# 128 instead of 64 tokens with gathered experts, and the choice of experts by head, among 112 pairs, with keys looked up in half precision

## The chip, the core and the metric

The kernel runs on one core of a Trainium2 chip. TensorE (PE) multiplies matrices, VectorE (DVE), ScalarE (ACT) and GpSimd (POOL) work on tensors, SyncE (SP) issues the large loads; sixteen DMA engines serve the core. The metric is the device time of one execution in microseconds (us), less is better. The median of three runs is quoted.

## The reference

Four layers of mixers and feed-forward blocks come first, then a block of sparse attention and a layer called `peer`, which the change is in. There are 512 tokens of width 1024. Each token chooses, in each of 8 heads, 16 of 16384 experts; an expert is one row of `u` and one of `v`.

```python
def peer(hn, w_q, subkeys, u, v):
    ...
    q = (xt @ w_q).reshape(T, H, 2, PEER_QDIM // 2)
    s = jnp.einsum('thcd,cnd->thcn', q, subkeys).astype(jnp.float32)
    s1, i1 = lax.top_k(s[:, :, 0], K)
    s2, i2 = lax.top_k(s[:, :, 1], K)
    cand = (s1[..., :, None] + s2[..., None, :]).reshape(T, H, K * K)
    sc, ci = lax.top_k(cand, K)
    e1 = jnp.take_along_axis(i1, ci // K, axis=-1)
    e2 = jnp.take_along_axis(i2, ci % K, axis=-1)
    idx = e1 * PEER_NKEYS + e2
    g = jax.nn.softmax(sc, axis=-1)
    ...
        a = jnp.einsum('cd,chkd->chk', xc, u[ic])
        act = (jax.nn.gelu(a.astype(jnp.float32)) * gc).astype(xc.dtype)
        return jnp.einsum('chk,chkd->cd', act, v[ic])
```

Here H is 8, K is 16, PEER_NKEYS is 128.

## The kernel before

Each engine runs its own hand-written list of instructions and waits on semaphores for the others. Weights come as a stream of slots of 128 x 1024 f32 (512 KB): SyncE loads a slot into one of four places of `ring`, ScalarE scales it (L1322) and makes its f16 high part (L1325), and GpSimd (L522) or VectorE (L2493, `weights_low`) subtracts to make the low part. TensorE multiplies a slot in 24 matmuls (L692 to L694), eight pieces with three products each. High parts are made two slots ahead of TensorE (`AHEAD`).

The `peer` stage computes most tokens densely, against all 16384 experts with gates that are zero for those not chosen, and the first `SPARSE` tokens by gathering the rows of their chosen experts. Its parts, in TensorE's order:

- queries: 8 slots, one output tile of 128 x 512 for each head, then one slot with the keys and 16 tiles of key scores (L1178), one for each group of 128 tokens, half of the heads and half of the key. ScalarE copies these to `key_scores`.
- `up0`: 32 slots of `u` for the dense tokens (448 columns). Beside it VectorE chooses the experts: for each of four groups of 128 tokens it takes the 16 best of 16 score lists (L2348, L2349, L2351 in `choose`), adds all 256 pairs for 8 heads (L1850), takes the 16 best of each, and finds the keys' numbers by comparing, multiplying and adding up in f32 (L2397, L1847, L2400).
- `up1a`: the first `U1_FIRST` slots of the second quarter of `u`. Then TensorE waits for `s_top`, transposes the choices (L1275), and goes on with `up1b`, the other slots of that quarter. Their results lie where `key_scores` lay, so ScalarE waits for the choice too (`s_diff`).
- `dn0`, `up2`, `dn1`, `up3`, `dn2`, `dn3`: 32 slots each, `dn` with rows of `v`. In `up1b`, `dn0`, `dn1` and `dn2`, the gated stretches, gates of the next quarter are made: VectorE builds one-hot vectors (L2455, L2459, L2463) for 8 tokens at a time, two such batches for a block of 16 tokens, TensorE spreads them (L1219), VectorE multiplies (L2474) and, when ScalarE has rounded (L1735), subtracts (L2484). In these stretches VectorE makes the low parts as well. In `up2`, `up3` and `dn3` GpSimd makes them.

The gathered tokens are a second, slower stream beside this. Two times 64 tokens stand on the 128 partitions (`FOLD` = 2), so 64 gathers bring their `u` rows and 64 their `v` rows. GpSimd issues a gather (L578), and VectorE takes one step with it: a dot product (L2514, `sparse_step`, with `u`) or a multiply-add (L2522, with `v`). The row buffers are `gathered`; a gather waits until the step that frees its buffer is done. `STEPS` says how many steps lie in each of the seven stretches from `up1b` to `dn3`. At slot 24 of `dn3` TensorE waits for the last step and folds the result into place (L1259), and VectorE adds it to x.

Of the kernel before, what the change touches and what calls it, by code (L numbers as in the profile page):

```python
# [21 lines left out]
T = 512  # L22
D = 1024
P = 128
C = D // P
# [21 lines left out]
SPARSE = 64  # L47
# [4 lines left out]
U1_FIRST = 12  # L52


STEPS = (4, 10, 36, 14, 36, 10, 18)
LAST_STEPS = 22
GATHERS = 3
# [23 lines left out]
for _k, _w in VEC_WIDTHS.items():  # L81
# [33 lines left out]
def build(nc, wstream, u_rows, v_rows, ada, ada_first, vecs, mats, phase, x_in, positions, out, stages):  # L115
# [4 lines left out]
    with ctx:  # L120
# [255 lines left out]
        half2 = rows[:, part_rows:part_rows + 31, :].rearrange("p c t -> p (c t)")  # L376
        key_scores = half2[:, 0:16 * T].rearrange("p (b h c n) -> p b h c n", b=TB, h=PEER_H, c=2)
        cand = half2[:, 16 * T:20 * T].rearrange("p (h n) -> p h n", h=PEER_H)
        match = half2[:, 20 * T:24 * T].rearrange("p (h k a) -> p h k a", h=PEER_H, k=PEER_K)
        pick = half2[:, 24 * T:28 * T].rearrange("p (a n) -> p a n", n=P)  # L380
        top_v = half2[:, 24 * T:24 * T + 256].rearrange("p (h c k) -> p h c k", h=PEER_H, c=2)
        top_i = half2[:, 24 * T + 256:25 * T].bitcast(u32).rearrange("p (h c k) -> p h c k", h=PEER_H, c=2)
        top_f = half2[:, 25 * T:25 * T + 256].rearrange("p (h c k) -> p h c k", h=PEER_H, c=2)
        best_v, best_i = pick[:, 6, :], pick[:, 7, :].bitcast(u32)
        digit_i, digit_f = pick[:, 8, :].bitcast(u32), pick[:, 9, :]

        expert = [half2[:, (28 + i) * T:(29 + i) * T].rearrange("p (b n) -> p b n", b=TB) for i in range(3)]
# [130 lines left out]
        def _(pool):  # L518
# [43 lines left out]
            first = n_slots - slots_of(stages[-1]) + 9 + E2_PART + U1_FIRST  # L562
# [35 lines left out]
        def _(pe):  # L598
# [560 lines left out]
            def experts():  # L1159
# [7 lines left out]
                linear([h16[:, k] for k in range(C)], 8, begun=2)  # L1167

                pe.wait_ge(s_evac, seen["tile"])
                w = ring[:, slot(), :]  # L1170
                for tb in range(TB):
                    for four in range(4):

                        b = bank()
                        half = slice(64 * (four % 2), 64 * (four % 2) + 64)
                        for i in range(4):
                            hd = 4 * (four // 2) + i
                            mm = nc.tensor.matmul(b[:, i * P:i * P + P], arena[half, hd, tb * P:tb * P + P],  # L1178
                                                  w[half, 0:P], start=True, stop=True)
                        mm.then_inc(s_used if tb == TB - 1 and four == 3 else s_tile, 1)  # L1180
# [129 lines left out]
        def _(act):  # L1310
# [396 lines left out]
            def experts():  # L1707
                split_input(None, y, peer_norm(seen)[0], C - 2)
                for m in range(8):
                    weighted(arena[:, m, :], 1)  # L1710
                    if m == 1:
# [6 lines left out]
                for tb in range(TB):  # L1718
                    for four in range(4):
                        b = tile(int(tb == TB - 1 and four == 3))  # L1720
                        nc.scalar.activation(key_scores[:, tb, 4 * (four // 2):4 * (four // 2) + 4, four % 2, :],
                                             b.rearrange("p (i n) -> p i n", i=4), ACT.Copy,
                                             scale=1.0 / W_SCALE).then_inc(s_evac, 1)
# [37 lines left out]
                act.wait_ge(s_diff, 3)  # L1761
# [6 lines left out]
                act.wait_ge(s_diff, TB)  # L1768
# [63 lines left out]
        def _(dve):  # L1832
# [521 lines left out]
            def experts():  # L2354
# [449 lines left out]
```

## Time and profile before

| | |
|---|---|
| median of three runs | 4963.15 us (4958.84 to 4964.7) |
| the profiled execution's own time | 4963.22 us |
| its span in the trace | 4961.4 us |
| PE, DVE, ACT, POOL busy in the span | 92%, 46%, 51%, 32% |
| mean granted TensorE clock | 0.942 |
| `peer` from `up0` on | 3585 us to 4958 us |

Rows of the timeline begin with the start and the length in us, then engine, line and operation, what is written and read with shapes, the count merged into the row, and in brackets the idle time before it and what ended it. Rows of windows give the stretch, its length, the busy us of PE, of PE's weight loads, DVE, ACT and POOL with their counts, the granted clock of TensorE, the busy share of the DMA engines and GB/s. Rows of groups give busy us and the mean ns of one, then the idle time before and its causes. An engine's next instruction starts up to 0.08 us before the record of the last one ends, so a price is read from start to start where it can be.

### The profile page before, as it was taken

Reading aid. Unit: us, or ns where it says so; the run is one execution under the profiler, and the core shown is the slowest. Engines: PE = TensorE matmul, PEld = TensorE weight load, DVE = VectorE, ACT = ScalarE, POOL = GpSimd, SP = SyncE. Lnnn points to the kernel's source line nnn. Section 1 sums busy time; section 2 is a strip of 40 time slices with the busy share of each in tenths; the row PEclk is TensorE's granted clock in tenths of the full one; section 3 lists DMA queues with packets and bytes.
Section 4 is the critical chain, followed back from the end, with each engine's and each line's share of the span. In section 5 each row is a group of like instructions: output and inputs, shape, how many; then the busy total and the mean of one; then the engine's idle time right before and its main releaser. Section 6 shows DMA issues by size and latency. Waiting matters only on the chain.

```text
span 4961.4 us, 67071 instructions
## 1 busy us (share of the span) xinstructions
PE 4545.2 (92%) x24838; PEld 2310.2 (47%) x24838; DVE 2306.9 (46%) x4495; ACT 2532.9 (51%) x3546; POOL 1598.9 (32%) x793
## 2 busy tenths in 40 slices
PE   3889999989989989997999999988997799999999
PEld 2454444544444434443444444454453455555555
DVE  4554221444233424414421023175299897595781
ACT  2457444557544445744466444464554445545444
POOL 1134432024433324432134433301353004517325
PEclk9889989999989999998899997988998999999999
DMA  3246222026322224521022322200232235647545
GB/s 144 89 161 254 94 83 72 1 84 255 111 87 81 72 71 160 218 99 63 25 78 97 102 85 81 85 5 26 82 115 89 78 114 178 223 133 224 175 133 165
DMA packets 142242, 557.42 MB, mean 112 GB/s; under 512 B 15792, under 2 KB 15920, under 8 KB 138528
## 3 DMA queue, kind: packets, MB, share of 16 engines
q1 hardware_dynamic: 123264, 484.11, 28.6%
q0 software_dynamic: 18720, 69.69, 4.4%
q8 instruction: 184, 3.01, 0.2%
q14 instruction: 74, 0.61, 0.0%
HBM read 551.64 MB, written 2.10 MB: 112 GB/s over the span
## 4 chain that ended last, share of the span: by engine, by line
PE 64%; issue 14%; DVE 14%; ACT 3%; POOL 3%; DMA 1%; SPq 0%; POOLq 0%; ACTq 0%; DVEq 0%
PE ps L692 17%; PE ps L693 17%; PE ps L694 17%; POOL halves L522 2%; PE ps L743 2%; DVE rows L2455 2%; DVE halves L2493 1%; DVE lasting L2474 1%; DVE rows L2463 1%; ACT halves L1325 1%; PE ps L888 1%; ACT ring L1322 1%; PE ps L878 1%; PE ps L699 1%; PE ps L700 1%
## 5 line engine op out<-in xcount | busy, mean ns | idle before, releaser
L522 POOL TENSOR_TENSOR halves<-ring,halves 128x1024 f16<-128x1024 f32 x603 | 1362.7, 2261 | 2580.0 <-ACT halves L1325 2574.0
L692 PE MATMUL ps<-h,halves 128*128 128x512 f16 (+1 forms) x2912 | 1090.1, 374 | 48.4 <-DVE h L1962 20.3
L693 PE MATMUL ps<-h,halves 128*128 128x512 f16 (+1 forms) x2912 | 1089.7, 374 | 0.0
L694 PE MATMUL ps<-h,halves 128*128 128x512 f16 (+1 forms) x2912 | 1088.5, 374 | 0.0
L692 PE MATMUL ps<-rows,halves 128*128 128x512 f16 (+2 forms) x2544 | 942.6, 371 | 80.0 <-DVE rows L1921 44.0
L1322 ACT ACTIVATE ring<-ring 128x1024 f32<-128x1024 f32 x719 | 754.1, 1049 | 441.0 <-DMA ring<-wstream 429.8
L693 PE MATMUL ps<-rows,halves 128*128 128x512 f16 (+2 forms) x2544 | 941.9, 370 | 0.0
L694 PE MATMUL ps<-rows,halves 128*128 128x512 f16 (+2 forms) x2544 | 941.1, 370 | 0.0
L1325 ACT ACTIVATE halves<-ring 128x1024 f16<-128x1024 f32 x719 | 759.8, 1057 | 22.8
L692 PEld LDWEIGHTS ps<-h,halves 128*128 128x128 f16 x2912 | 287.3, 99 | 384.6 <-issue 60.3
L694 PEld LDWEIGHTS ps<-h,halves 128*128 128x128 f16 x2912 | 287.8, 99 | 325.2 <-issue 15.1
L693 PEld LDWEIGHTS ps<-h,halves 128*128 128x128 f16 x2912 | 287.1, 99 | 313.7 <-issue 13.2
L692 PEld LDWEIGHTS ps<-rows,halves 128*128 128x128 f16 x2544 | 252.4, 99 | 347.2 <-DVE rows L1921 46.7
L694 PEld LDWEIGHTS ps<-rows,halves 128*128 128x128 f16 x2544 | 252.8, 99 | 272.7 <-issue 12.7
L693 PEld LDWEIGHTS ps<-rows,halves 128*128 128x128 f16 x2544 | 252.4, 99 | 254.2 <-issue 10.1
L2111 DVE TENSOR_TENSOR rows<-rows 128x512 f32 x128 | 94.2, 736 | 401.3 <-ACT rows L1503 401.3
L1850 DVE TENSOR_TENSOR rows<-rows,h 128x512 f32<-128x512 f32 x40 | 29.4, 736 | 465.9 <-ACT h L1398 465.4
L578 POOL DMA_INDIRECT rows<-u_rows,h x64 | 82.4, 1287 | 486.6 <-DVE h L2514 436.8
L1735 ACT ACTIVATE rows<-lasting 128x512 f32 (+1 forms) x112 | 70.5, 629 | 317.2 <-DVE lasting L2474 317.2
L1727 ACT ACTIVATE rows<-ps 128x448 f32 (+1 forms) x128 | 69.4, 543 | 252.3 <-PE ps L694 252.2
L1355 ACT ACTIVATE rows<-ps 128x512 f32<-128x512 f32 x136 | 78.1, 595 | 188.8 <-PE ps L694 188.5
L1398 ACT ACTIVATE h<-ps 128x512 f32<-128x512 f32 x64 | 38.2, 597 | 260.0 <-PE ps L694 260.0
(265 smaller groups left out, 5499.3 us busy)
## 6 DMA issues: line engine op xcount, KB each, us to landing
ring<-wstream SPq DMA_DIRECT2D x719, 512.0 KB, 3.3
rows<-ada SPq DMA_DIRECT2D x96, 768.0 KB, 4.8
rows<-ada_first SPq DMA_DIRECT2D x24, 1024.0 KB, 5.7
x<-x_in POOLq DMA_DIRECT2D x1, 2048.0 KB, 14.0
out<-x SPq DMA_DIRECT2D x8, 256.0 KB, 4.5
rows<-phase_nsa SPq DMA_DIRECT2D x1, 1600.0 KB, 6.6
rows<-phase_ret SPq DMA_DIRECT2D x1, 1024.0 KB, 4.9
rows<-u_rows,h POOLq DMA_INDIRECT x64, 5.3
```

Source lines behind the costliest of these rows:

```text
L522: nc.gpsimd.tensor_tensor(halves[:, j % RING, 1, :], ring[:, j % RING, :], halves[:, j % RING, 0, :], ALU.subtract).then_inc(s_wlow, 1)
L578: nc.gpsimd.indirect_dma_start(gathered[n % GATHERS], None, table, index)\
L692: nc.tensor.matmul(out_, high, act16[:, 0, :], start=first, stop=False)
L693: nc.tensor.matmul(out_, high, act16[:, 1, :], start=False, stop=False)
L694: return nc.tensor.matmul(out_, low, act16[:, 0, :], start=False, stop=last)
L743: mm = nc.tensor.matmul(ps[:, g % 3, 0:sg.keys], a, b, start=(k == 0), stop=(k == len(sg.products) - 1))
L1322: nc.scalar.activation(ring[:, at % RING, :], ring[:, at % RING, :], ACT.Copy, scale=W_SCALE).then_inc(s_wscaled, 1)
L1325: nc.scalar.activation(halves[:, at % RING, 0, :], ring[:, at % RING, :], ACT.Copy).then_inc(s_whigh, 1)
L1355: nc.scalar.activation(dst, b, func, scale=scale / W_SCALE).then_inc(s_evac, 1)
L1735: nc.scalar.activation(acts16[:, lo:lo + E2_PART, 0, bass.ds(i * HALF + j, 1), :] .rearrange("p e o t -> p e (o t)"), gated[j % 2], ACT.Co ...
L2111: nc.vector.tensor_tensor(chunk[:, 1, :], (rinv, tmp)[j % 2][:, :], chunk[:, 0, :], ALU.subtract).then_inc(s_hidl, 1)
L2455: nc.vector.tensor_tensor(hot1[:, n].rearrange("p t (e o) -> p t e o", o=2), key_pairs(0, P, pairs), token_pairs(buf, 0, n, pairs), ALU.is ...
```

## The change

It does four things.

1. `SPARSE` is 128: the dense tokens are 384 and not 448, `FOLD` is 1, and there are 128 gathers of `u` rows and 128 of `v` rows. `GATHERS`, the number of row buffers, is 6 and not 3. `STEPS` is (10, 28, 56, 34, 60, 28, 40) for (4, 10, 36, 14, 36, 10, 18). A gated stretch has 24 blocks of 16 tokens for 28.
2. The keys are a constant loaded with the others, so their slot falls away, and the key scores are computed head by head among the queries.
3. VectorE chooses by head for all 512 tokens, adds and searches 112 of the 256 pairs, and looks the keys' numbers up twice, four heads at a time, in f16.
4. `U1_FIRST` is 2 and not 12.

```diff
-SPARSE = 64
+SPARSE = 128
-U1_FIRST = 12
-STEPS = (4, 10, 36, 14, 36, 10, 18)
-LAST_STEPS = 22
-GATHERS = 3
+U1_FIRST = 2
+STEPS = (10, 28, 56, 34, 60, 28, 40)
+LAST_STEPS = 24
+GATHERS = 6
...
+CANDS = 4 * PEER_K + 4 * (PEER_K - 4)
+def head_order():
+    order = [("q", 0), ("q", 1), ("s", 0), ("s", 1), ("q", 2)]
+    for m in range(3, PEER_H):
+        order += [("q", m), ("s", m - 1)]
+    return order + [("s", PEER_H - 1)]
...
                 for kind, m in head_order()[2:]:
+                    if kind == "q":
+                        linear([h16[:, k] for k in range(C)], m + 1, begun=m)
+                    else:
+                        pe.wait_ge(s_evac, t0 + head_tiles(("q", m)))
+                        for c in range(2):
+                            b = bank()
+                            half = slice(64 * c, 64 * c + 64)
+                            for tb in range(TB):
+                                mm = nc.tensor.matmul(b[:, tb * P:tb * P + P], arena[half, m, tb * P:tb * P + P],
+                                                      keys[half, :], start=True, stop=True)
+                            mm.then_inc(s_tile, 1)
...
-                act.wait_ge(s_diff, 3)
+                act.wait_ge(s_diff, 2)
...
+                for hd in range(PEER_H):
+                    at = hd % 4
+                    dve.wait_ge(s_evac, t0 + head_tiles(("s", hd)))
+                    choose(lambda i: top_v[:, at, i // 2, i % 2, :], lambda i: top_i[:, at, i // 2, i % 2, :],
+                           lambda i: key_scores[:, hd, i % 2, i // 2, :], 2 * TB)
+                    for low, high, width, lo in ((0, 4, PEER_K, 0), (4, PEER_K, 3, 4 * PEER_K)):
...
+                        link(add(pairs[:, :, :, 0:width], firsts.to_broadcast(shape), seconds.to_broadcast(shape)))
+                    choose(lambda i: best_v[:, at, i, :], lambda i: best_i[:, at, i, :], lambda i: cand[:, i, :], TB)
+                    if at < 3:
+                        continue
...
+                    for i in range(2):
...
+                        link(nc.vector.tensor_tensor(match.rearrange("p n (q o) -> p n q o", o=2), digit, places,
+                                                     ALU.is_equal))
...
+                        link(mul(by_list, by_list, keys))
+                        for n in (8, 4, 2):
+                            link(add(match[:, :, 0:n], match[:, :, 0:n], match[:, :, n:2 * n]))
```

VectorE's order where the choice begins, before: the last half of the layer's input, the fold matrix (L2367, L1850), and then all 16 score lists of the first 128 tokens at once. The names are tiles, `rows` holds the scores and the choices.

```order
L1959 TENSOR_TENSOR h<-rows,h 128x512 x2
L2367 COPY h<-lasting 128x2x32
L1850 TENSOR_TENSOR h<-h,lasting 128x2x32
L2348 MAX rows<-rows 128x8 x16
L2349 MAX_INDEX rows<-rows 128x8 x16
L2351 MATCH_REPLACE rows<-rows 128x128 x16
```

The same place in the changed kernel, where L2375, L2376 and L2378 are the lines of `choose`, and L1877 adds pairs.

```order
L1986 TENSOR_TENSOR h<-rows,h 128x512 x2
L2386 CAST scalars<-rows 128x128
L2387 CAST rows<-rows 128x16
L2389 MEMSET rows 128x4x12
L2375 MAX rows<-rows 128x8 x8
L2376 MAX_INDEX rows<-rows 128x8 x8
L2378 MATCH_REPLACE rows<-rows 128x128 x8
...
L1877 TENSOR_TENSOR rows<-rows 128x4x64
L1877 TENSOR_TENSOR rows<-rows 128x4x12x3
L2375 MAX rows<-rows 128x8 x4
L2376 MAX_INDEX rows<-rows 128x8 x4
L2378 MATCH_REPLACE rows<-rows 128x112 x4
```

The fold matrix has moved behind the choice, and a search covers the 8 lists of one head, then its 4 lists of pairs. Before, one lookup on VectorE for 128 tokens (it stands eight times) reads:

```order
L2392 TENSOR_SCALAR rows<-rows 128x128
L2393 CAST rows<-rows 128x128
L2397 TENSOR_TENSOR rows<-rows 128x2048
L1847 TENSOR_TENSOR rows<-rows 128x2048
L2400 TENSOR_REDUCE rows<-rows 128x128
```

Of the change, one lookup for four heads and all tokens (it stands four times); before each second one stand nine small instructions (L2416 to L2433).

```order
L2438 TENSOR_TENSOR rows<-rows 128x4096
L1874 TENSOR_TENSOR rows<-rows 128x4096
L1877 TENSOR_TENSOR rows<-rows 128x256x8
L1877 TENSOR_TENSOR rows<-rows 128x256x4
L1877 TENSOR_TENSOR rows<-rows 128x256x2
L1877 TENSOR_TENSOR rows<-rows 128x4x16 x4
```

One compare and one multiply now cover twice the elements, and the reduction has become three halvings and four small additions. On GpSimd, where `up2` ends, `dn1` passes with gathers alone and `up3` begins with the first low part behind them, before:

```order
L522 TENSOR_TENSOR halves<-ring,halves 128x1024
L578 DMA rows<-u_rows,h 128x1024 x13
L578 DMA rows<-v_rows,h 128x1024 x3
L522 TENSOR_TENSOR halves<-ring,halves 128x1024
L578 DMA rows<-v_rows,h 128x1024
```

The same place in the changed kernel, with L550 the low part and L606 the gather:

```order
L606 DMA rows<-u_rows,h 128x1024 x2
L550 TENSOR_TENSOR halves<-ring,halves 128x1024
L606 DMA rows<-u_rows,h 128x1024 x30
L606 DMA rows<-v_rows,h 128x1024 x6
L550 TENSOR_TENSOR halves<-ring,halves 128x1024
L606 DMA rows<-v_rows,h 128x1024
L550 TENSOR_TENSOR halves<-ring,halves 128x1024
L606 DMA rows<-v_rows,h 128x1024 x2
```

There are now more than twice as many gathers in `dn1`, and mostly two behind a low part of `up3`, where one stood.

## Rows read from the trace of the kernel before

**Rows 1.** The stretches up0, up1a, up1b, dn0, up2, dn1, up3, dn2, dn3, by windows.

```profile
3585.00:3730.00 145.00, 145.00 (x768) 75.02 (x767) 140.63 (x559) 88.55 (x102) 76.26 (x33) 1.00 0.35 116
3730.00:3820.00 90.00, 58.97 (x302) 30.80 (x299) 85.96 (x273) 35.17 (x49) 29.68 (x13) 0.83 0.23 76
3820.00:3984.00 164.00, 125.98 (x1377) 69.39 (x1378) 141.69 (x339) 70.21 (x95) 8.07 (x6) 0.95 0.27 84
3984.00:4160.00 176.00, 171.88 (x1657) 97.39 (x1658) 162.67 (x364) 79.81 (x90) 14.25 (x10) 0.98 0.38 124
4160.00:4305.00 145.00, 145.00 (x780) 75.14 (x777) 64.79 (x78) 82.10 (x97) 112.14 (x67) 1.00 0.74 240
4305.00:4483.00 178.00, 171.87 (x1652) 97.45 (x1650) 166.18 (x370) 81.30 (x92) 22.50 (x16) 0.98 0.43 142
4483.00:4629.00 146.00, 145.59 (x785) 75.31 (x783) 70.51 (x43) 82.71 (x98) 121.92 (x67) 1.00 0.76 239
4629.00:4809.00 180.00, 171.86 (x1669) 97.70 (x1668) 165.46 (x357) 83.83 (x95) 15.60 (x12) 0.98 0.40 131
4809.00:4958.00 149.00, 149.00 (x784) 77.39 (x782) 34.16 (x28) 62.02 (x59) 85.89 (x46) 0.98 0.51 168
```

**Rows 2.** Timeline of PE at the head of the stage and at the wait.

```profile
3542.57 1.04 PE L1164 MATMUL ps<-lasting,rows 128*64 128x128 f32 x8
...
3575.38 9.47 PE L1178 MATMUL ps<-ring,rows 64*128 64x128 f32 x128 [0.69 <-ACT rows L1355]
...
3816.51 2.82 PE L1275 MATMUL ps<-lasting,rows 128*128 128x128 f32 x12 [23.48 <-DVE rows L1847]
3820.30 0.56 PE L692 MATMUL ps<-h,halves 128*128 128x448 f16 x1 [0.97 <-DVE rows L2417]
```

**Rows 3.** Timeline of ACT: the first query tile copied.

```profile
3544.66 0.58 ACT L1355 ACTIVATE rows<-ps 128x512 f32<-128x512 f32 x1
```

**Rows 4.** Timeline of DVE: the choice for the first 128 tokens.

```profile
3589.39 3.19 DVE L2348 MAX8 rows<-rows 128x8 f32<-128x128 f32 x16
...
3608.76 2.29 DVE L1850 TENSOR_TENSOR rows<-rows 128x2048 f32<-128x2048 f32 x1
...
3626.43 0.29 DVE L2384 TENSOR_TENSOR rows<-rows 128x128 f32<-128x128 f32 x1
...
3629.81 4.10 DVE L1847 TENSOR_TENSOR rows<-rows 128x2048 f32<-128x2048 f32 x1
```

**Rows 5.** Timeline of DVE: the end of the choice, TensorE idle.

```profile
3809.42 2.29 DVE L1847 TENSOR_TENSOR rows<-rows 128x2048 f32<-128x2048 f32 x1
...
3814.07 0.23 DVE L2401 CAST scalars<-rows 128x128 f16<-128x128 f32 x1
```

**Rows 6.** Timeline of DVE in dn0: a step, a low part, a block.

```profile
4041.50 1.22 DVE L2514 CUSTOM_DVE_ANT_0 rows<-rows 128x1024 f32<-128x1024 f32 x1
...
4042.64 1.22 DVE L2493 TENSOR_TENSOR halves<-ring,halves 128x1024 f16<-128x1024 f32 x1
...
4046.31 0.22 DVE L2442 COPY scalars<-rows 128x128 f16<-128x128 f16 x1
...
4051.57 0.22 DVE L2442 COPY scalars<-rows 128x128 f16<-128x128 f16 x1
```

**Rows 7.** Groups of POOL in up2, then of POOL and DVE in up3.

```profile
L522 POOL TENSOR_TENSOR halves<-ring,halves 128x1024 f16<-128x1024 f32 x32 | 72.0, 2250 | 22.0 <-ACT halves L1325 21.7
L578 POOL DMA_INDIRECT rows<-u_rows,h x35 | 41.2, 1176 | 20.8 <-ACT halves L1325 15.2 <-issue 3.1
...
L522 POOL TENSOR_TENSOR halves<-ring,halves 128x1024 f16<-128x1024 f32 x32 | 74.1, 2317 | 12.9 <-ACT halves L1325 12.5
L578 POOL DMA_INDIRECT rows<-v_rows,h x35 | 48.6, 1390 | 14.7 <-DVE h L2514 8.9 <-issue 4.8
...
L2522 DVE SCALAR_TENSOR_TENSOR rows<-rows,h 128x1024 f32<-128x1024 f32 x35 | 65.4, 1869 | 72.4 <-DMA rows<-v_rows,h 71.8
```

**Rows 8.** Timeline of POOL in up2: a short gather.

```profile
4256.22 0.95 POOL L578 DMA_INDIRECT rows<-u_rows,h  x1
```

More of the change, by code:

```diff
@@ L381, in build @@
[L381 to L387, printed above, removed]
+        half2 = rows[:, part_rows:part_rows + 29, :].rearrange("p c t -> p (c t)")
@@ L560, in _ @@
                 updates += 1
-            first = n_slots - slots_of(stages[-1]) + 9 + E2_PART + U1_FIRST
+            first = n_slots - slots_of(stages[-1]) + 8 + E2_PART + U1_FIRST
             lows(done, first + AHEAD)
@@ L1166, in experts @@
                 mm.then_inc(s_nat, 1)
[L1167 to L1180, printed above, removed]
+                t0 = seen["tile"] - 2
+                pe.wait_ge(s_phase, seen["phase"])
+                keys = const("peer", "keys")
+                for kind, m in head_order()[2:]:
+                    if kind == "q":
[9 more added lines that the diff above has]
+                            mm.then_inc(s_tile, 1)
                 def up(i, j, t0, n0, after=lambda k: None):
@@ L1708, in experts @@
                 split_input(None, y, peer_norm(seen)[0], C - 2)
-                for m in range(8):
-                    weighted(arena[:, m, :], 1)
-                    if m == 1:
+                for kind, m in head_order():
+                    if kind == "q":
+                        weighted(arena[:, m, :], 1)
+                    else:
+                        for c in range(2):
+                            copy(key_scores[:, m, c, :, :].rearrange("p b n -> p (b n)"))
+                    if (kind, m) == ("s", 1):
                         act.wait_ge(s_nat, 1)
@@ L2401, in experts @@
[L2401 to L2403 removed]
+                link(nc.vector.tensor_copy(iota_h, iota))
+                link(nc.vector.tensor_copy(iota16_h, iota16))
+                link(nc.vector.memset(cand[:, :, 4 * PEER_K:CANDS].rearrange("p b (i j) -> p b i j", j=4)[:, :, :, 3:4],
+                                      LOWEST))
+                t0 = seen["tile"] - 8
@@ new lines, in experts @@
+                for f in range(FOLD):
+                    part = ident[:, f * SPARSE:(f + 1) * SPARSE].rearrange("p (a t) -> p a t", a=2)
+                    if f == 0:
+                        nc.vector.tensor_copy(fold, part).then_inc(s_fold, 1)
+                    else:
+                        dve.wait_ge(s_fold, f)
+                        add(fold, fold, part).then_inc(s_fold, 1)
+                link(nc.vector.scalar_tensor_tensor(out=sparse_pick, in0=expert[0][:, 0, :], scalar=float(NKEY),
@@ L2780, in arrays_of @@
     for kind in PHASE_WIDTHS:
[L2781 removed]
+        out[f"phase_{kind}"] = phase_constants(kind, a)
     return out
```

129 lines of the change are left out of this document (66 added, 63 removed).

## The prediction

> **What bounds the kernel now.** I read the windows of the `peer` stage first, since nothing ahead of it changes. Nine stretches follow each other from 3585 to 4958 us [rows 1]. In `up0`, `up2` and `up3` TensorE is busy from end to end at full clock: 145 us for 32 slots, 4.54 us a slot. In `dn0`, `dn1` and `dn2` it is busy 172 of 176 to 180 us, and VectorE 163 to 166 us, so TensorE sets the pace with VectorE close behind: 32 slots at 4.54 are 145, and the other 31 us are the gates' matmuls. `dn3` is TensorE's again. Two stretches are not TensorE's. `up1a` has 12 slots, 54.5 us of work, and lasts 90: the timeline of PE has it idle for 23.5 us until VectorE has chosen [rows 2], and the rest of the loss is ahead of that, where ScalarE may not yet write over the scores; the granted clock falls to 0.83. `up1b` lasts 164 us with PE busy 126 and DVE 142, where 20 slots must carry all gates of a quarter [rows 1].
>
> The other resources have room before. In `up2` and `up3` GpSimd is busy 112 and 122 us and the DMA engines 0.74 and 0.76 of the time, with 67 transfers of 512 KB each: 32 slots and 35 gathers [rows 1, 7].
>
> **The dense matmuls.** Six query tiles of 512 columns fill 3543.6 to 3574.7 us, 5.18 us each [rows 2]; 448 columns cost 4.54. The 64 columns between are worth 0.64, so 384 columns cost 3.90 us a slot, 124.8 us for 32. If TensorE alone decided, the 256 slots would give 164 us. The rest of the working is on how much of it the others let through.
>
> **The head of the stage.** The query tiles 0 and 1 end at 3542.6 us, the transposes near 3543.6. The first scores need ScalarE's copy of tile 0, which ends at 3545.2 [rows 3]; TensorE waits some 2 us, and about 1 more for the last head. The 128 score matmuls remain, 9.5 us for all [rows 2], and their slot had hidden loads. I put the begin of `up0` at 3587.5 instead of 3584.8: 2.7 us lost.
>
> **The choice.** It began behind all scores, at 3587.6 and, with the fold matrix done, at 3589.4 [rows 4]. Now it begins when the first head's eight matmuls (0.6 us) are copied (1.1 us for two): 3547.3. TensorE makes a head in 5.8 us, and VectorE needs far longer, so it never waits again. A search of 16 lists of 128 took 3589.39 to 3608.76, 19.4 us; 8 lists are half and a little for the waits between, 10.0. Eight lists of 256 took, behind the 2.29 of adding pairs, 15.3 us to 3626.43 [rows 4], so a list costs 1.21 at 128 and 1.92 at 256, and at 112 by the line through both 1.12; 4 lists with the waits are 4.9. Adding pairs, 256 and 144 elements instead of 2048 at 2.29, is 0.8. A head is 15.7 us, eight are 126.
>
> The lookup in f16 has no row. Per four heads I count 5 us for the thirteen small instructions, and two lookups. A compare of 4096 f16 elements has the bytes of 2048 f32 ones; the multiply of that size took 2.29 us beside an idle TensorE [rows 5] and 4.10 beside a busy one [rows 4]. I take 2.29 for the compare, 4.10 for the multiply, which keeps its shape and company, and for halvings and small additions 3.2: 9.6 us, 24.3 for four heads, 49 in all. The bounds: all at the speed of the idle rows, 7 us less; each large instruction at one f16 element for one f32 element, so twice as long, 30 us more. The Trainium skill, VectorE: DVE Perf Modes, section on the perf-mode tier table, has a two-input operation on 16-bit operands at twice the f32 rate, 2.29 us for each large one; by it alone the choice would end 7 us earlier. The f32 row that took 4.10 shows that such a rate need not be met here.
>
> With the tail (3814.1 to 3816.5 before, 2.5 us) `s_top` comes at 3547.3 + 126 + 49 + 2.5 = 3725. TensorE has done its 34 slots at 3587.5 + 34 x 3.90 = 3720, so a wait of 5 us is left. ScalarE needs `s_diff` at 3700 only, ahead of that. Transposes and copies take 3.8 us (3816.5 to 3820.3 [rows 2]), so `up1b` begins at 3729 for 3820: 91 us gained, of which 39 are the ten slots moved behind (at 3.90). The shorter choice, in f16 and over fewer pairs, is worth this much only together with `U1_FIRST`.
>
> **The gated stretches.** VectorE's prices are read from start to start [rows 6]: a low part 1.14, a step 1.14, a block 5.26 less the low part in it, 4.12. The eight additions to x of a stretch have under half of a low part's elements; I put them at 0.5 each. `dn0` is then 24 x 4.12 + 32 x 1.14 + 8 x 0.5 + 28 x 1.14 = 99 + 36 + 4 + 32 = 172 us, `dn1` with 34 steps 178, `dn2` 172. TensorE would need 124.8 + 31 x 24/28 = 151. So VectorE becomes the bound: its load before was 168 (10 steps). It waits also for ScalarE inside a block; before, 8 us lay between that load and the 176 of the stretch, part of it TensorE's. I add 7: 179, 185, 179, where 176, 178, 180 stood. The gain of 64 columns is given back in full, 9 us more.
>
> `up1b` has 30 slots and 10 steps: VectorE 99 + 34 + 11 = 144, TensorE 117 + 27 = 144. Before, VectorE's 143 took 164, with 1.4 blocks a slot; now there are 0.8, as in `dn`. I take 156, between 145 and 165.
>
> **The stretches in which GpSimd makes the low parts.** `up2` has 56 gathers, `up3` 60. GpSimd needs 2.25 us for a low part and 1.18 for a gather, 2.32 and 1.39 in `up3` [rows 7], and some 0.16 between two, an estimate from the issue gaps there (4.8 us for 35 gathers in `up3`). 32 x 2.41 + 56 x 1.34 = 152 us, and 32 x 2.48 + 60 x 1.55 = 172. The DMA engines: 0.74 x 145 / 67 = 1.60 us of all sixteen for a transfer, so 88 need 141 us; 0.76 x 146 / 67 = 1.66, so 92 need 152 [rows 1]. Both are over TensorE's 125. A low part is queued behind up to two gathers, and TensorE waits for it. I take 154 and 168; before 145 and 146. `dn3`: 24 slots with 34 gathers still to issue are about 104 us for GpSimd against 94, then 8 slots and the fold, 34: 138 for 149. Six buffers instead of three take away VectorE's waits for rows, 72 us in `up3` [rows 7], but these were hidden.
>
> **Sum.** 3729 + 156 + 179 + 154 + 185 + 168 + 179 + 138 = 4888, plus 3 us for storing: a span of 4891 for 4961.4. By stretches, up to `up1b` -91, then -8, +3, +9, +7, +22, -1, -11: -70 us, 1.4%. The profiled execution's own time is 1.8 us over its span and 0.1 over the median, so 4893 us; I say 4895.
>
> **The rivals.**
> - Forecast, 0.57. Its own range by the bounds: `up1b` 145 to 165, the `dn` 172 to 187 each, the `up` 141 to 160 and 150 to 180: 4845 to 4940.
> - TensorE keeps the pace in `up2`, `up3` and `dn3`, 0.18. Many gathers are as short as 0.95 us [rows 8], and GpSimd idled 33 us of `up2` (145 less 112). With gathers at 0.95 plus 0.16, and the low parts as before, it needs 139 and 146 us; where VectorE's steps then leave it alone and the low parts get shorter too, TensorE's 125 comes into reach. 22 us less in `up2` and 32 in `up3`, half way between, and 9 in `dn3`: 4832, from 4815 on.
> - Lookups at the full price, 0.12: `s_top` at 3755, TensorE idle 35 us, and a clock that is low behind it as in `up1a` (0.83 [rows 1]): 4930.
> - Slower, 0.13: VectorE and GpSimd get in each other's way. A step is 1.2 us alone and 1.87 on average in `up3` [rows 7], beside a busy GpSimd. In the gated stretches GpSimd issues 100 gathers instead of 38; if each step there costs 1.87 and no longer 1.14, it is 100 x 0.73 = 73 us more, all on VectorE, the bound: 4968, and with a gather at 1.76 instead of 1.18 to 1.39 in `up2` and `up3` another 54: over 5000. It decides from 0.8 us a step on. Against it, the steps of `dn0` stand at 1.22 beside the ten gathers there. The Trainium skill, GPSIMD Engine Reference, Specifications, says that GpSimd's SBUF interfaces are shared with VectorE, with contention at instructions with two SBUF inputs, which every step is; the 1.87 agrees.
>
> **How the numbers follow.** The likeliest case gives 4895. To leave out no more than 2 in 10 the range goes down to the lower part of the second case and up over the third to where the fourth begins: 4825 to 4955. A measurement of this kernel tells about 0.2%, 10 us, from no change. Faster by more than that: the first three and a third of the fourth, 0.87 with some loss for what I have not seen, 0.86. Within 0.2%: 0.05. Slower: 0.09.
>
> **What would show it.** `up1b` begins near 3729, with an idle time ahead of the transposes of 5 us, not 23.5. The gated stretches have DVE busy over 0.93 and PE busy some 151 of 180. `up2` and `up3` last over 150 with PE idle for GpSimd's low parts and a DMA share over 0.9; if they last 125 to 130, GpSimd's prices were taken too high. If the `dn` stretches last 160, VectorE's load was. If the steps in them are longer than 1.3 us, the last rival is at work.

## The result, and the profile after

The kernel before takes 4962.99 us (median of 4 runs, 4958.84 to 4964.7), the changed kernel 4909.93 us (4906.72 to 4913.52): a ratio of 0.9894, interval 0.9877 to 0.9912. It is 53 us faster, where 68 were forecast, and inside the range.

The first view is the windows of the nine stretches of the changed kernel, in the order of [rows 1]. The columns are the same: the window and its length, the busy time of PE, PEld, DVE, ACT and POOL, TensorE's granted clock, the DMA share and GB/s.

```profile
3590.00:3715.00 125.00, 125.00 (x772) 75.22 (x771) 122.17 (x542) 85.52 (x101) 69.89 (x32) 1.00 0.40 132
3715.00:3749.00 34.00, 11.21 (x64) 7.31 (x63) 30.35 (x65) 10.31 (x20) 5.59 (x3) 0.70 0.14 47
3749.00:3906.00 157.00, 139.65 (x1487) 87.57 (x1484) 142.38 (x313) 90.50 (x116) 22.06 (x15) 1.00 0.47 152
3906.00:4075.00 169.00, 151.41 (x1539) 93.67 (x1540) 164.97 (x355) 77.36 (x86) 39.85 (x27) 0.98 0.58 180
4075.00:4240.00 165.00, 133.56 (x768) 74.53 (x767) 97.14 (x122) 82.39 (x100) 149.22 (x85) 0.97 0.83 273
4240.00:4414.00 174.00, 150.85 (x1537) 92.47 (x1537) 171.56 (x362) 76.65 (x86) 52.90 (x36) 0.99 0.64 203
4414.00:4585.00 171.00, 131.45 (x769) 73.48 (x770) 104.61 (x71) 80.82 (x98) 153.14 (x91) 0.99 0.84 280
4585.00:4761.00 176.00, 150.23 (x1537) 92.75 (x1534) 171.94 (x332) 80.81 (x90) 46.82 (x32) 0.98 0.61 190
4761.00:4909.00 148.00, 131.18 (x784) 76.33 (x784) 79.89 (x51) 62.34 (x60) 118.28 (x65) 0.99 0.71 239
```

Three things are to be seen. Up to `up1b` the stage has become 71 us shorter; 39 of these are the ten slots, 3.90 us each, that `up1b` now has more. In the gated stretches DVE is now the busiest engine (172 of 174 us in `dn1`), with PE at 150 to 151. In `up2` and `up3` TensorE is busy at most 134 of 165 and 171 us, against 145 of 145 before, and POOL 149 and 153. Against forecast, in us; the last column is measured from TensorE's first matmul of a stretch to its first one of the next:

| | before | forecast | after |
|---|---|---|---|
| `up1b` begins at | 3820 | 3729 | 3748.6 |
| `up1b` | 164 | 156 | 157.6 |
| `dn0` | 176 | 179 | 168.5 |
| `up2` | 145 | 154 | 165.3 |
| `dn1` | 178 | 185 | 174.1 |
| `up3` | 146 | 168 | 170.9 |
| `dn2` | 180 | 179 | 176.2 |
| `dn3` | 149 | 138 | 147.6 |

The timeline of PE where the choice ends, to be held against the last rows of [rows 2]:

```profile
3744.77 2.82 PE L1305 MATMUL ps<-lasting,rows 128*128 128x128 f32 x12 [21.82 <-DVE rows L1874]
3748.56 0.34 PE L720 MATMUL ps<-h,halves 128*128 128x384 f16 x1 [0.97 <-DVE rows L2474]
```

The wait is still there, 21.8 us for 23.5, although 71 us earlier and behind only 2 slots of `up1`.

The first lookup stands under GpSimd's low parts. The timeline of DVE there, and below it that of POOL:

```profile
3620.77 4.10 DVE L2438 TENSOR_TENSOR rows<-rows 128x4096 f16<-128x4096 f16 x1
3624.91 4.11 DVE L1874 TENSOR_TENSOR rows<-rows 128x4096 f16<-128x4096 f16 x1
3629.05 7.24 DVE L1877 TENSOR_TENSOR rows<-rows 128x2048 f16<-128x2048 f16 x7
```

```profile
3620.39 2.34 POOL L550 TENSOR_TENSOR halves<-ring,halves 128x1024 f16<-128x1024 f32 x1 [1.78 <-ACT halves L1355]
3624.28 2.58 POOL L550 TENSOR_TENSOR halves<-ring,halves 128x1024 f16<-128x1024 f32 x1 [1.56 <-ACT halves L1355]
3628.18 2.83 POOL L550 TENSOR_TENSOR halves<-ring,halves 128x1024 f16<-128x1024 f32 x1 [1.32 <-ACT halves L1355]
```

The second lookup comes when GpSimd has hardly any work left. DVE's timeline:

```profile
3726.16 2.29 DVE L2438 TENSOR_TENSOR rows<-rows 128x4096 f16<-128x4096 f16 x1
3728.49 2.29 DVE L1874 TENSOR_TENSOR rows<-rows 128x4096 f16<-128x4096 f16 x1
3730.82 3.46 DVE L1877 TENSOR_TENSOR rows<-rows 128x2048 f16<-128x2048 f16 x7
```

The same three rows cost 15.5 and 8.0 us. GpSimd's low part ends at 3622.73, and VectorE's compare 2.14 later, at 3624.87; the next low part seems to run from there, 3624.87 to 3626.86, and the multiply ends 2.16 behind it. As I read these rows, the two engines take turns, and the recorded spans include the waiting. `e10_narrow_lows` below tests whether GpSimd is the cause.

The groups of `up2`, which answer to the first rows of [rows 7] (busy us, mean ns, idle time ahead):

```profile
L606 POOL DMA_INDIRECT rows<-u_rows,h x54 | 80.2, 1485 | 17.2 <-issue 10.8 <-DVE h L2571 3.1 <-ACT halves L1355 2.7
L550 POOL TENSOR_TENSOR halves<-ring,halves 128x1024 f16<-128x1024 f32 x31 | 69.0, 2227 | 0.6
L2571 DVE CUSTOM_DVE_ANT_0 rows<-rows 128x1024 f32<-128x1024 f32 x58 | 93.3, 1628 | 65.3 <-DMA rows<-u_rows,h 65.1
```

GpSimd no longer waits for ScalarE's halves (0.6 us ahead of its low parts, 22.0 before), and a gather takes 1.49 us for 1.18. The waits of the same stretch (engine and line, waited for: us, times, longest) say who pays:

```profile
PE ps L720 <- POOL halves L550: 31.0, 20, 2.4
```

In `dn0`, DVE's groups show the steps undisturbed:

```profile
L2550 DVE TENSOR_TENSOR halves<-ring,halves 128x1024 f16<-128x1024 f32 x31 | 37.8, 1218 | 0.0
L2571 DVE CUSTOM_DVE_ANT_0 rows<-rows 128x1024 f32<-128x1024 f32 x28 | 34.1, 1218 | 0.0
L2512 DVE TENSOR_TENSOR rows<-scalars 128x1024 f16<-128x1024 f16 x48 | 32.9, 686 | 2.2 <-PE ps L1249 1.3
...
L2556 DVE SCALAR_TENSOR_TENSOR x<-ps,x 128x384 f32<-128x384 f32 x7 | 3.9, 552 | 0.0
```

Hardly a group waits (2.2 us at most): VectorE is the bound there. The timeline of POOL has two kinds of gathers in this stretch, and that of DVE shows what stands beside each:

```profile
3947.66 1.68 POOL L606 DMA_INDIRECT rows<-u_rows,h  x1 [3.13 <-DVE h L2571]
3954.06 0.94 POOL L606 DMA_INDIRECT rows<-u_rows,h  x1 [4.72 <-DVE h L2571]
```

```profile
3947.30 1.22 DVE L2550 TENSOR_TENSOR halves<-ring,halves 128x1024 f16<-128x1024 f32 x1
3954.18 1.21 DVE L2550 TENSOR_TENSOR halves<-ring,halves 128x1024 f16<-128x1024 f32 x1
```

The first gather starts inside a low part of VectorE and ends 0.8 us behind it; the second starts just ahead of one and is short. Of the 27 gathers recorded in `dn0`, 19 are of the first kind and take 1.68 us, 7 are of the second and take 0.94. The low parts take 1.22 us at most, also where a gather began before them.

### The profile page after: what moved, and what is told of

It is laid out like the page before. It is cut to its first block, busy times and chain, and to the rows that moved or that the text cites. A ratio compares the mean times of both kernels' runs of the same rounds, so it can differ in the third digit from the quotient of the medians.

```text
span 4911.7 us, 66130 instructions
## 1 busy us (share of the span) xinstructions
PE 4389.7 (89%) x24326; PEld 2291.1 (47%) x24326; DVE 2406.8 (49%) x4548; ACT 2512.6 (51%) x3525; POOL 1767.7 (36%) x910
## 4 chain that ended last, share of the span: by engine, by line
PE 52%; DVE 19%; issue 14%; POOL 10%; ACT 3%; DMA 1%; SPq 0%; POOLq 0%; DVEq 0%; ACTq 0%
PE ps L720 13%; PE ps L722 13%; PE ps L721 13%; POOL halves L550 6%; POOL rows L606 3%; DVE halves L2550 2%; DVE rows L2512 2%; PE ps L771 2%; DVE rows L2571 1%; DVE rows L2520 1%; DVE lasting L2531 1%; DVE rows L2376 1%; PE ps L916 1%; DVE rows L2541 1%; PE ps L906 1%
## 5 line engine op out<-in xcount | busy, mean ns | idle before, releaser
L550 POOL TENSOR_TENSOR halves<-ring,halves 128x1024 f16<-128x1024 f32 x592 | 1330.2, 2248 | 2473.5 <-ACT halves L1355 2471.3
L720 PE MATMUL ps<-h,halves 128*128 128x512 f16 (+1 forms) x2912 | 1062.7, 365 | 110.5 <-POOL halves L550 72.0
L721 PE MATMUL ps<-h,halves 128*128 128x512 f16 (+1 forms) x2912 | 1061.5, 365 | 0.0
L722 PE MATMUL ps<-h,halves 128*128 128x512 f16 (+1 forms) x2912 | 1060.5, 364 | 0.0
L720 PE MATMUL ps<-rows,halves 128*128 128x512 f16 (+2 forms) x2544 | 914.8, 360 | 91.4 <-DVE rows L1948 44.0
L721 PE MATMUL ps<-rows,halves 128*128 128x512 f16 (+2 forms) x2544 | 913.6, 359 | 0.0
L722 PE MATMUL ps<-rows,halves 128*128 128x512 f16 (+2 forms) x2544 | 913.1, 359 | 0.0
L606 POOL DMA_INDIRECT rows<-u_rows,h x128 | 188.6, 1473 | 409.1 <-DVE h L2571 362.4
L1877 DVE TENSOR_TENSOR rows<-rows,h 128x512 f32<-128x512 f32 x40 | 29.4, 736 | 465.9 <-ACT h L1428 465.4
L2579 DVE SCALAR_TENSOR_TENSOR rows<-rows,h 128x1024 f32<-128x1024 f32 x127 | 207.1, 1631 | 89.0 <-DMA rows<-v_rows,h 84.5
L606 POOL DMA_INDIRECT rows<-v_rows,h x128 | 178.8, 1397 | 171.0 <-DVE rows L2579 132.0
L1763 ACT ACTIVATE rows<-lasting 128x512 f32 (+1 forms) x96 | 60.5, 630 | 320.3 <-DVE lasting L2531 316.4
L2571 DVE CUSTOM_DVE_ANT_0 rows<-rows 128x1024 f32<-128x1024 f32 x128 | 178.4, 1404 | 65.3 <-DMA rows<-u_rows,h 65.1
```

Of the source, the lines that this page charges most:

```text
L550: nc.gpsimd.tensor_tensor(halves[:, j % RING, 1, :], ring[:, j % RING, :], halves[:, j % RING, 0, :], ALU.subtract).then_inc(s_wlow, 1)
L606: nc.gpsimd.indirect_dma_start(gathered[n % GATHERS], None, table, index)\
L720: nc.tensor.matmul(out_, high, act16[:, 0, :], start=first, stop=False)
L721: nc.tensor.matmul(out_, high, act16[:, 1, :], start=False, stop=False)
L722: return nc.tensor.matmul(out_, low, act16[:, 0, :], start=False, stop=last)
L2571: ins = nc.vector.tensor_tensor_reduce(out=row, in0=row, in1=sparse_in, scale=1.0, scalar=0.0, op0=ALU.mult, op1=ALU.add, accum_out=column ...
```

## The experiments

Ratios are to the kernel before, with their intervals. The first four change one part each.

**The choice alone** (`e1_choice_only`): the changed kernel with the old number of tokens and all that hangs on it. **The tokens alone** (`e2_tokens_only`): the kernel before with the opposite edit, `U1_FIRST` 12.

```diff
-SPARSE = 128
-STEPS = (10, 28, 56, 34, 60, 28, 40)
-LAST_STEPS = 24
-GATHERS = 6
+SPARSE = 64
+STEPS = (4, 10, 36, 14, 36, 10, 18)
+LAST_STEPS = 22
+GATHERS = 3
```

> The changed kernel with SPARSE = 64, STEPS, LAST_STEPS and GATHERS as before, so the choice by head alone (with U1_FIRST = 2). Theory (the choice brings the gain, 128 tokens give theirs back in the gated stretches and lose in up2 and up3): up1b begins near 3749 as in the changed kernel; up1b about 175, dn0, dn1, dn2 176 to 179, up2 and up3 145, dn3 150: 4890 to 4915, not slower than the changed kernel's 4910. Rival (the 64 columns fewer on TensorE bring a part of the gain): over 4925.

> The kernel before with SPARSE = 128, STEPS, LAST_STEPS and GATHERS of the change, so the 128 tokens alone, with the old choice and U1_FIRST = 12. Theory: the choice ends near 3816 as before, up1b about 150, and from dn0 on the 1003 us of the changed kernel for 974 before: 4960 to 4985, no gain or a loss against 4963. Rival (128 tokens bring a gain of their own): under 4945.

Measured: the choice alone 4900.23 us, 0.9872 (0.9856 to 0.9889); the tokens alone 4972.49 us, 1.0018 (1.0009 to 1.0028). So the choice and `U1_FIRST` bring 63 us, and the 64 further tokens cost 9 or 10 on either footing. The parts add up: -63 and +9 are -54, measured -53. The gain of the change is that of its choice with `U1_FIRST`, and the rest of it is a small loss. How much the earlier begin, the 112 pairs, f16, the keys' slot and `U1_FIRST` bring each, no run separates.

**A share of the low parts for VectorE** (`e3_low_share`): in `up2`, `up3` and `dn3` VectorE makes every fourth low part, 23 instead of 31 left on GpSimd in `up2`.

```diff
-                    if own and first + s + AHEAD < n_slots:
+                    if own and first + s + AHEAD < n_slots and s % SHARE != 1:
+                        if s % SHARE == 2:
+                            pool.wait_ge(s_wlow, first + s + AHEAD)
                         weights_low(first + s + AHEAD)
...
+                        for s in range(E2_PART):
+                            if s % SHARE == 1:
+                                weights_low(at + s + AHEAD)
+                            for _ in due(s, E2_PART, STEPS[2 * part]):
+                                sparse_step()
```

> The changed kernel with every fourth low part of up2, up3 and dn3 made by VectorE. Theory (GpSimd's time sets these stretches, 149 and 153 us busy of 165 and 171): GpSimd has 8 x 2.4 = 19 us less in each, VectorE 9 more of which it has room for: up2 about 148, up3 155, dn3 141, 4870 in all. Rival (the DMA engines set them, 137 and 144 us of packets at a share of 0.83): within 8 us of 4910.

Measured: 4882.55 us, 0.9837 (0.982 to 0.9853); `up2` 152.1, `up3` 156.4, `dn3` 140.8 us. Fewer operations on GpSimd shorten the stretches while the same bytes go through the DMA queues, so it is GpSimd's time that sets them. `up3` and `dn3` are within 1.4 us of the 155 and 141 expected, `up2` is 4 us above its 148. In the waits of `up2` VectorE, which makes its low part in turn behind GpSimd's, now waits for GpSimd; that this is where the 4 us went was not tried. The three stretches win 34.5 us in the profiled executions, the medians differ by 27.

```profile
DVE halves L2553 <- POOL halves L551: 44.9, 8, 7.6
```

**Steps with one input** (`e4_one_input`): the steps over `u` read only the gathered row.

```diff
-                        ins = nc.vector.tensor_tensor_reduce(out=row, in0=row, in1=sparse_in, scale=1.0, scalar=0.0,
-                                                             op0=ALU.mult, op1=ALU.add, accum_out=column(sums_s, k))
+                        ins = nc.vector.tensor_reduce(out=column(sums_s, k), in_=row, axis=AX.X, op=ALU.add)
```

> The changed kernel with the dot product of each u step replaced by a sum over the gathered row, an instruction with one tensor input and the same 1024 elements; it leaves out the product with the token. Theory (two-input instructions of VectorE and GpSimd's work exclude each other in time): in up2 a step falls from 1.64 to 1.22 us, a gather from 1.49 to about 1.1, the stretch from 165 to about 148, up3 with its v steps stays at 171: about 4893. Rival (a gather is as long by itself, or VectorE disturbs it with any instruction): up2 stays at 160 to 166, 4905 to 4912.

Measured: 4884.3 us, 0.9841 (0.9825 to 0.9857); `up2` 134.7 us for 165.3, while `up3`, whose steps are over `v`, stays at 171.2 as the control. The groups of `up2`:

```profile
L2571 DVE TENSOR_REDUCE h<-rows 128x1 f32<-128x1024 f32 x58 | 70.2, 1218 | 60.6 <-DMA rows<-u_rows,h 56.6 <-issue 3.7
L550 POOL TENSOR_TENSOR halves<-ring,halves 128x1024 f16<-128x1024 f32 x31 | 66.4, 2142 | 0.8 <-issue 0.2
L606 POOL DMA_INDIRECT rows<-u_rows,h x54 | 51.9, 962 | 17.3 <-issue 10.5 <-DVE h L2571 3.9 <-ACT halves L1355 2.7
```

The number of GpSimd's instructions is that of the changed kernel, and a gather has fallen from 1.49 to 0.96 us. The step has fallen with it (1.63, now 1.22). So VectorE's step is what lengthened the gather. The edit takes two things from the step, its second input and the 1024 results that it writes back; which of them counts, this run does not say, but `e8_psum` does, whose steps over `u` still write theirs.

**Other numbers of steps** (`e5_steps`) moves steps out of `up2` and `up3` into the gated stretches.

```diff
-STEPS = (10, 28, 56, 34, 60, 28, 40)
+STEPS = (16, 34, 36, 42, 44, 42, 42)
```

> The changed kernel with STEPS = (16, 34, 36, 42, 44, 42, 42): 20 steps moved out of up2 into up1b, dn0 and dn1, 16 out of up3 into dn2 and dn3. Theory (a step costs VectorE 1.14 to 1.2 us in a gated stretch, and GpSimd about 1.6 with its gather in up2 and up3): up1b +7, dn0 +7, up2 165 to about 137, dn1 +9, up3 171 to about 148, dn2 +16, dn3 +3: about 4901. Rival (the gated stretches have room left for steps, TensorE's 151 setting them): under 4880.

Measured: 4902.32 us, 0.988 (0.9863 to 0.9896). `up2` and `up3` win 28.5 and 18.9 us, `dn1` and `dn2` lose 9.5 and 15.9, `dn0` 5.6, `up1b` and `dn3` 3 each: what is taken off GpSimd goes to VectorE, which is the bound there.

**Three row buffers** (`e7_three_buffers`):

```diff
-GATHERS = 6
+GATHERS = 3
```

> The changed kernel with 3 row buffers instead of 6. Theory (in up2 and up3 a buffer is taken for the 6 us from issue to landing and for the step, some 9 us in all, so three allow one step each 3 us, 165 to 180 us for 56 to 60): 4915 to 4950. Rival (GpSimd's time alone counts, the buffers don't): 4905 to 4913.

Measured: 4949.51 us, 0.9976 (0.9965 to 0.9988); from `up2` on every stretch is longer, `up3` by 14, the others by 3.5 to 5.5. GpSimd idles 21.8 us of `up2` until a step frees a buffer, for 3.1 with six. By the medians, six buffers are worth 40 us with 56 and 60 steps in a stretch.

**The second input in PSUM** (`e8_psum`): in `up2`, `up3` and `dn3` the gated product's input and the running sum lie in two free banks, with a copy on the way in and the last step writing back. The whole computation stands.

```diff
+                in_psum = ps[:, 6:8, :].rearrange("p b t -> p (b t)")
+                ups = [range(sum(STEPS[:i]), sum(STEPS[:i + 1])) for i in (2, 4, 6)]
...
+                    if n == ups[0].start:
+                        link(nc.vector.tensor_copy(in_psum, sparse_in))
+                    read = in_psum if inside and n not in (ups[1].start, ups[2].start) else sparse_in
+                    write = in_psum if inside and n not in (ups[1][-1], ups[2][-1]) else sparse_in
```

> The changed kernel with the second operand of the steps of up2, up3 and dn3 (the tokens for u, the running sum for v) kept in two free PSUM banks instead of SBUF, the whole computation kept. Theory (only two operands in SBUF make VectorE and GpSimd exclude each other): steps at 1.2 to 1.3 us, gathers at 0.96 and low parts at 2.14 as in the run with a one-input step; up2 135, up3 about 140, dn3 about 133: 4830 to 4845. Rival (it is the product as such, or the write to SBUF beside it, that excludes): up3 at 165 or more, over 4880.

Measured: 4840.91 us, 0.9752 (0.9736 to 0.9768); `up2` 134.4, `up3` 142.1, `dn3` 133.3 us. The groups of `up2`:

```profile
L2581 DVE CUSTOM_DVE_ANT_0 rows<-rows,ps 128x1024 f32<-128x1024 f32 x56 | 68.0, 1221 | 58.1 <-DMA rows<-u_rows,h 57.6
L550 POOL TENSOR_TENSOR halves<-ring,halves 128x1024 f16<-128x1024 f32 x31 | 66.5, 2144 | 0.6
L606 POOL DMA_INDIRECT rows<-u_rows,h x54 | 51.8, 958 | 17.3 <-issue 9.3 <-DVE h L2581 5.3 <-ACT halves L1355 2.7
```

and the window of the stretch:

```profile
4079.00:4213.00 134.00, 126.94 (x766) 73.14 (x766) 74.66 (x121) 82.19 (x97) 117.82 (x85) 1.00 0.92 332
```

It is `e4_one_input` over again with nothing left out. The steps of `up2` still write 1024 results to SBUF (`rows<-rows,ps`); what has changed is where their second input lies. POOL's busy time falls by 31 us (149.2 to 117.8) for the same work, and so does the stretch. The DMA engines now run at 0.92 and 332 GB/s, which shows that they were not the bound at 0.83.

**PSUM, and five slots of `up1` ahead of the choice's end** (`e9_psum_u1`): `e8_psum` with one line more.

```diff
-U1_FIRST = 2
+U1_FIRST = 5
```

> The run with the second operand in PSUM, and U1_FIRST = 5 besides, so that three more slots stand ahead of TensorE's 21.8 us of waiting for the choice. Theory (up1b is paced by VectorE, so what moves out of it is worth three low parts at 1.14 us): 2 to 5 us below the run with U1_FIRST = 2. Rival (TensorE's time counts, 3 x 3.90): 12 us below it.

Measured: 4840.97 us, 0.9757 (0.974 to 0.9773), no gain. `up1a` and `up1b` together take 193.9 us for 194.5. `up1b` does get shorter, 154.4 us for 160.5, which is 6 us and more than the expectation had. But TensorE still waits 14.9 us (22.3 in `e8_psum`), because the choice ends 5.4 us later: three more low parts on GpSimd reach into the lookup behind the last four heads. The timeline of DVE there:

```profile
3727.45 4.10 DVE L2438 TENSOR_TENSOR rows<-rows 128x4096 f16<-128x4096 f16 x1
3731.58 4.12 DVE L1874 TENSOR_TENSOR rows<-rows 128x4096 f16<-128x4096 f16 x1
3735.74 5.26 DVE L1877 TENSOR_TENSOR rows<-rows 128x2048 f16<-128x2048 f16 x7
3741.04 2.29 DVE L2438 TENSOR_TENSOR rows<-rows 128x4096 f16<-128x4096 f16 x1
```

In `e8_psum` the first three of these rows are 2.29, 2.29 and 3.46 us. As the rows read, the 6 us that `up1b` gains are lost again to the same collision as in the first lookup; no run has the one without the other.

**GpSimd's low parts narrowed under the choice** (`e10_narrow_lows`): 64 of 1024 columns in `up0` and `up1a`.

```diff
-                nc.gpsimd.tensor_tensor(halves[:, j % RING, 1, :], ring[:, j % RING, :], halves[:, j % RING, 0, :],
-                                        ALU.subtract).then_inc(s_wlow, 1)
+                wide = 64 if narrow else SLOT
+                nc.gpsimd.tensor_tensor(halves[:, j % RING, 1, 0:wide], ring[:, j % RING, 0:wide],
+                                        halves[:, j % RING, 0, 0:wide], ALU.subtract).then_inc(s_wlow, 1)
```

> The changed kernel with GpSimd's low parts of the slots of up0 and up1a 64 instead of 1024 columns wide; it leaves out the rest of these low parts. Theory (the first lookups are long because GpSimd's work and VectorE's two-input instructions exclude each other: 40 us against 24.3 for the second ones, beside which GpSimd has nothing to do): the first group's compare and multiply fall from 4.1 to 2.3 us, the choice ends 16 to 20 us earlier, up1b begins near 3730: about 4892. Rival (they are long because TensorE and ScalarE are busy): 4.1 us as before, over 4905.

Measured: 4894.12 us, 0.9861 (0.9845 to 0.9878). The timelines of DVE at the first lookup and behind the last, and of PE at the wait:

```profile
3615.00 2.29 DVE L2440 TENSOR_TENSOR rows<-rows 128x4096 f16<-128x4096 f16 x1
3617.32 2.29 DVE L1876 TENSOR_TENSOR rows<-rows 128x4096 f16<-128x4096 f16 x1
...
3723.46 0.69 DVE L2467 TENSOR_REDUCE rows<-rows 128x32 f32<-128x512 f32 x1 [7.63 <-ACT rows L1798]
...
3725.32 2.82 PE L1307 MATMUL ps<-lasting,rows 128*128 128x128 f32 x12 [4.43 <-DVE rows L1876]
```

TensorE is as busy with `up0` as in the changed kernel (124.8 us in both), and yet compare and multiply take 2.29 us. So the 4.10 is GpSimd's doing, not TensorE's. From VectorE's first search to the end of the last lookup it is 168.8 us for 193.8, 25 less. VectorE then waits 7.6 us for ScalarE, so `up1b` begins only 19.4 us earlier (3729.1 for 3748.6, and forecast at 3729), 2 of which `up0` was early already in this run; 16 reach the end.

**PSUM and other numbers of steps** (`e11_psum_steps`): `e8_psum` with steps moved into `up1b` and `dn3`.

```diff
-STEPS = (10, 28, 56, 34, 60, 28, 40)
+STEPS = (18, 28, 52, 30, 54, 24, 50)
```

> The run with the second operand in PSUM, with STEPS = (18, 28, 52, 30, 54, 24, 50): steps moved out of up2 and up3, which the DMA engines now set (0.92 and 0.93 busy, 1.4 us for a gather), and out of dn1 and dn2 (VectorE, 1.14 and 1.2 us) into up1b, where 6 more cost 3 us or nothing, and into dn3, where GpSimd and the DMA engines have room. up2 134 to 130, dn1 175 to 171, up3 142 to 134, dn2 175 to 170, up1b +4, dn3 +3: 4820 to 4830. Rival (dn3 and up1b have no room left for steps): 4838 or more.

Measured: 4831.78 us, 0.9736 (0.972 to 0.9752), the best version: 2.6% under the kernel before and, by the two medians, 1.6% under the changed one. Each of `up2` to `dn2` wins 3 to 7 us; `dn3` loses 9, not 3, to its ten more steps. Its time lies 2 us over what was expected.

## Why the prediction held, and where its terms were off

**Up to `up1b`: -91 forecast, -71 measured.** The mechanism holds: the choice begins with the first head and runs under `up0`. The begin was forecast at 3547.3 and is 3548.6, VectorE's first search. A head was to cost 15.7 us and costs 16.3 (64.1 for the first four, 66.2 for the last), 5 us in all. The lookup behind the last four costs its 24.3 to the digit (3718.12 to 3742.45), but by luck, because two errors cancel: I had 4.10 for the multiply, which is 2.29 away from GpSimd, and 5 for the small instructions, which take 8.0. Two of these meet GpSimd's last two low parts:

```profile
3721.36 2.24 DVE L2432 CAST rows<-rows 128x512 f16<-128x512 f32 x1
3723.53 2.60 DVE L2433 TENSOR_TENSOR rows<-rows 128x512 f16<-128x512 f32 x1
```

In `e10_narrow_lows` they take 0.43 and 0.69, and all of the small ones 4.3 us. The lookup behind the first four costs 39 (3612.7 to 3651.9), 15 too much. The term that was off is "4.10 beside a busy one": I laid the slow multiply of [rows 4] to TensorE. It is GpSimd that makes it slow, as `e10_narrow_lows` shows. The trace of before had it. Its timelines of POOL and DVE at that multiply, which I had not laid side by side:

```profile
3624.06 2.13 POOL L522 TENSOR_TENSOR halves<-ring,halves 128x1024 f16<-128x1024 f32 x1 [2.41 <-ACT halves L1325]
3628.60 3.17 POOL L522 TENSOR_TENSOR halves<-ring,halves 128x1024 f16<-128x1024 f32 x1 [2.41 <-ACT halves L1325]
```

```profile
3627.49 2.29 DVE L2397 TENSOR_TENSOR rows<-rows 128x2048 f32<-128x2048 f32 x1
3629.81 4.10 DVE L1847 TENSOR_TENSOR rows<-rows 128x2048 f32<-128x2048 f32 x1
```

VectorE's compare was first, from 3627.49 to 3629.78, and GpSimd's low part took 3.17 us instead of 2.13, as if it had begun behind it (3631.77 less 2.13 is 3629.64). The multiply then ended at 3633.91, which is 2.14 behind the low part. So of two such instructions the one that starts second ends its own length, less 0.14 or 0.15 us, behind the first. The rival "lookups at the full price" gave a late `s_top` (3755) from another cause, a halved rate, and is refuted by the 2.29 of the second lookup. The rate is that of the Trainium skill, VectorE: DVE Perf Modes, section on the perf-mode tier table: twice the f32 rate for a `tensor_tensor` on 16-bit operands, from which an estimate for 4096 f16 elements is 2.29 us. The trace agrees where GpSimd is away (2.29), and not beside its low parts (4.10).

**`U1_FIRST`.** "A wait of 5 us is left" failed with the same term: 21.8. By windows the granted clock is 0.60, between its levels of 1.2 and 2.4 GHz, while TensorE has next to nothing to do (3723 to 3745 us), and 1.00 from 3749 us on, and `up1b` lasted 157.6 for 156: the low clock did not outlast the wait by more than the transposes.

**`dn0`, `dn1`, `dn2`: together +9 us forecast, -15 measured.** That TensorE's gain from 64 fewer columns would be given back to VectorE was right in kind: DVE is busy 172 of 174 and 176 us in `dn1` and `dn2`. What failed is "I add 7": waits inside the blocks hardly exist once VectorE is the bound (2.2 us in `dn0`). The load itself was a little high in `dn0` and `dn1`: 172 and 178, where they last 168.5 and 174.1 (and 99 + 36 + 4 + 32 is 171). In `dn2` it was low, 172 for 176.2; 2 us of this are its 28 steps over `v`, at 1.28 us and not 1.22. The additions to x are the 0.5 each that I gave them (0.55 in the row above).

**`up2`, `up3`, `dn3`: +9, +22, -11 forecast; +20, +25, -1 measured.** GpSimd is the bound, as forecast (`e3_low_share`). In `up2` the size came from a gather at 1.18 us, and it was 1.49. More steps with more buffers meet GpSimd more often; that was not reckoned with, although the last rival named it. With three buffers and the same steps (`e7_three_buffers`) a gather of `up2` takes 1.31, so the number of steps and that of buffers seem to have a part each. In `up3` the rows' prices held (1.38 and 2.31 us), and the 172 of their sum was nearer to the 170.9 measured than the 168 that I took. `dn3` was priced at the rows of `up2`, 104 us for 24 slots; at those of `up3` it is 112 and 146 in all, near the 147.6. The DMA term came near for the load, 141 us against 0.83 of 165, which is 137; the share of over 0.9 did not come because the stretch was longer. As a bound it was wrong: in `e8_psum` the same transfers went through in 134.4 us.

**"But these were hidden."** The waits for rows, 72 us before, were not hidden once there were 56 to 60 steps: three buffers cost 40 us (`e7_three_buffers`).

**How much of it was luck.** TensorE's last slot ends at 4908.6 us for 4888. Later or longer than forecast were the begin of `up1b` (19.6 us), `up1b` (1.6), `up2` (11.3), `up3` (2.9) and `dn3` (9.6), 45 us in all; shorter were `dn0`, `dn1` and `dn2`, by 24. Without this second error, which has nothing to do with the first, 4910 would have been about 4934: still inside the range, but 39 us from 4895 and not 15.

**The rivals.** "TensorE keeps the pace" did not come true in the changed kernel, but its condition, gathers at 0.95 us and VectorE's steps leaving GpSimd alone, is what `e8_psum` makes (0.96), and its 4832 is near the 4841 measured, with the same two errors cancelling in the other stretches. "Slower" was right in its mechanism and wrong in its place: a step costs 1.63 us in `up2` and 1.218 in `dn0`. The gated stretches have gathers (27 recorded in `dn0`, 1.48 us each) but no low parts by GpSimd, and a gather did not lengthen VectorE's instructions: even in `up2`, where 34 steps started while a gather ran, their median is 1.22 us. Long are steps that meet GpSimd's low parts, up to 3.8. The rule of the Trainium skill, GPSIMD Engine Reference, Specifications, that it rests on (contention at instructions of VectorE with two SBUF inputs) is what `e4_one_input` and `e8_psum` show: with one SBUF input less the gather falls to 0.96 us in both.

## What to carry to other kernels

Where a VectorE instruction of one kind has two durations in a trace, lay GpSimd's timeline beside it before pricing a new one. If both engines must be busy, give VectorE's long two-input instructions their second operand in PSUM, if banks are free: it cost nothing per instruction and was worth 69 us here, more than the whole change. Work taken off TensorE is worth what the engines that take it over leave of it: 164 us of matmuls exchanged for 128 more steps and as many gathers made the kernel 9 us slower.

## What was not expected of the hardware

- VectorE's instructions with two inputs in SBUF and GpSimd's low parts excluded each other over whole instructions: 2.29 us became 4.10, 2.13 became 3.17.
- With gathers it went one way. A gather that started inside a low part of VectorE in `dn0` took 1.68 us instead of 0.94, and ended 0.8 us behind it; the low parts and steps did not wait for a gather. All 17 steps of `up2` over 1.4 us overlap a low part of GpSimd.
- Two inputs are not the only condition: a cast of 128 x 512 from f32 to f16 took 2.24 us beside a low part and 0.43 without. The searches of the choice took 0.28 us either way.
- A VectorE instruction of 1024 f32 elements took 1.22 us with its second input in SBUF or in PSUM alike.
- Gathers of 128 rows together with streamed weights moved 332 GB/s at a DMA share of 0.92 on one core.
- What stays open: which operands of VectorE's cast make it wait, and why a gather does not hold VectorE up as a low part does. The exclusion itself is shown by the three runs that take one side away (`e4_one_input`, `e8_psum`, `e10_narrow_lows`); that it goes by which instruction starts first is read from timelines, and no run changes that order alone.
